# Three gathers of each expert layer cut into 120 and 8 rows, between short copies that turn the ring of DMA engines

## The chip, the cores and the metric

The kernel runs on one core of a Trainium2 chip. The metric is the device time of one execution in microseconds (us); lower is better. The kernel before takes 2239.84 us, the median of three runs (2239.53 to 2241.55). A profile of one execution goes with it: its time was 2241.91 us and the span of its instructions 2240.1 us.

## What is computed

256 tokens of width 1024 pass a first transformer block (three kinds of attention, a gated feed-forward with a short convolution) and then two layers of a second block: attention, and an expert layer ("PEER"). The change touches the expert layer alone. Cut to that:

```python
def peer_ffn(x, w_query, sub_keys, expert_down, expert_up):
    def chunk(xc):                                   # 128 tokens
        q = (xc @ w_query).reshape(PEER_CHUNK, PEER_HEADS, 2, half)
        s = jnp.einsum('thpk,pnk->thpn', q, sub_keys)
        sv, si = lax.top_k(s, PEER_TOPK)             # 16 of 128 keys, twice
        cand = sv[:, :, 0, :, None] + sv[:, :, 1, None, :]
        cidx = si[:, :, 0, :, None] * PEER_N_KEYS + si[:, :, 1, None, :]
        ...
        top_s, sel = lax.top_k(cand, PEER_TOPK)      # 16 of 16 x 16 pairs
        eidx = jnp.take_along_axis(cidx, sel, axis=-1)
        g = jax.nn.softmax(top_s, axis=-1)
        u, vv = expert_down[eidx], expert_up[eidx]
        act = jax.nn.gelu(jnp.einsum('td,thkd->thk', xc, u), approximate=False)
        return jnp.einsum('thk,thkd->td', g * act, vv)
```

Every token takes 8 heads x 16 experts from 16384, and each expert is one row of `experts` with its down and up vectors side by side: 2 x 1024 floats, 8 KB.

## The kernel before

The kernel is written by hand for each engine: a program for SP (weight loads), POOL (gathers and small work), PE (matmuls), ACT and DVE, tied by semaphores. The order within an engine is the order in which its program is written; no planner is involved.

An expert layer works in 16 steps of 16 picks: `STEPS` = 2 tiles of 128 tokens x 8 heads. One step k has two passes c of `RING` = 8 picks each. For one pick of all 128 tokens of a tile, POOL issues one indirect DMA (`gather`, L1098): 128 rows of 8 KB from `experts` into slot r of `ring`, one row to each partition, with the row numbers in a column of `EIDX`. So there are 256 gathers in a layer, 512 in all. What follows for a slot, always in this order:

- DVE waits for `g_landed[r]` and takes the dot of the tokens with the down vectors (L2143 in step 0, L2166 later).
- ACT takes the gelu of it (L1667), times the gate (L1669), and puts it on a diagonal matrix (L1672).
- PE multiplies the diagonal with the up vectors into PSUM (`slot`, L1315) and raises `slot_used[r]`.
- POOL waits for `slot_used[r]` and issues the gather of the same slot for the next pass.

Eight slots thus bound how far POOL runs ahead. Between its dots DVE does the routing of the next step (top-16 of the keys, `paired` and `keyed`), which ends with the row numbers in `EIDX` (L2046) and raises `routed`; `gathers(k, b)` on POOL waits for that once per step. Steps 0 and 1 are written out on POOL, the others are a loop. In the first tile (k under 8) PE also does the rest of the query projections between the slots.

SP loads the weight halves in the order in which they are needed (`reload`, L1039). For the halves of layer 1 it waits, from the second half on, for the last gather of layer 0. After the last gather of a layer, PE closes the sums (L1323, L1327), DVE adds them to x (L484), and the next layer or the store of the result follows. The changed parts are the SP program (L1047 to L1066), `gathers` on POOL (L1102 to L1117), and `step_dve` on DVE (L2154 to L2200).

Of the kernel before, what the change touches and what calls it, by code (L numbers as in the profile page):

```python
# [83 lines left out]
PQ_FIRST = 3  # L84
DOTS_AHEAD = 2
PQ_MIXED = PH - PQ_FIRST
PQ_HELD = range(2 * PQ_FIRST + 1, 2 * PH)
# [66 lines left out]
def build(nc, x_in, wstream, consts, bands, par1, par2, na_bias, experts, out):  # L154
    ctx = ExitStack()
    with ctx:
# [3 lines left out]
        def sem(name):  # L160
            return ctx.enter_context(nc.semaphore(name))
# [12 lines left out]
        ZERO = sb("zero", [P, 512], BF16)  # L174
        EIDX = sb("expert_idx", [P, 2, TOPK], U32)
        GWT = sb("expert_gate", [P, 2, TOPK])
        work = sb("work", [P, 16392])
# [120 lines left out]
        topd_ready, texp_ready, routed, gates_ready = sem("topd_ready"), sem("texp_ready"), sem("routed"), sem("gates_ready")  # L298
        g_landed = [sem(f"g_landed{i}") for i in range(RING)]
        slot_used = [sem(f"slot_used{i}") for i in range(RING)]  # L300
        dots_ready, gelu_ready, w_ready, diag_ready = sem("dots_ready"), sem("gelu_ready"), sem("w_ready"), sem("diag_ready")
# [7 lines left out]

        class Norm:  # L310


            def __init__(self, name):
                self.sq = sem(name + "_squares")
                self.var = sem(name + "_var")
                self.std = sem(name + "_std")
                self.rstd = sem(name + "_rstd")
                self.hn = sem(name + "_normed")
                self.xp = sem(name + "_transposed")
                self.hi = sem(name + "_hi")  # L320
                self.hT = sem(name + "_hT")

        n_attn, n_post, n_ffn = Norm("n_attn"), Norm("n_post"), Norm("n_ffn")
        n_mix, n_peer = Norm("n_mix"), Norm("n_peer")

# [702 lines left out]
        def _(sp):  # L1028
# [13 lines left out]
            with sp.Fori(0, whole) as k:  # L1042
                for s in range(SLOTS):
                    sp.wait_ge(w_lo, k * SLOTS + s + 1)
                    sp.dma_start(W[:, s, :], wstream[k * SLOTS + SLOTS + s]).then_inc(w_landed[s], 16)
            for n in range(SLOTS + whole * SLOTS, HALVES):
                l, local = divmod(n - L_HALF, L_HALVES)  # L1047
                if held(n) is not None:
                    continue
                if n >= L_HALF + L_HALVES and 0 < local < SLOTS:  # L1050
                    sp.wait_ge(g_landed[RING - 1], l * USES * 16)
                reload(n)
                e = local - HELD_BESIDE
                if 0 <= e < len(PQ_HELD):
                    if e == 0:
                        sp.wait_ge(lpT_taken, l * L_FILLS + batches2[-1].values + 1)
                    gains_end = Q_QKN + (e - HELD_ARENA + 1) * HW - Q_GF
                    if gains_end > 0 and e >= HELD_ARENA:
                        sp.wait_ge(n_peer.hn, 4 * l + -(-min(gains_end, D) // GC))
                    sp.dma_start(held_place(e), wstream[L_HALF + l * L_HALVES + 2 * LG_PQ + PQ_HELD[e]]).then_inc(held_landed[e], 16)  # L1060
            sp.wait_ge(x_ready, 3 * LAYERS + 2 * TT - 1)
            sp.wait_ge(g_landed[RING - 1], LAYERS * USES * 16)
# [7 lines left out]
        def _(pool):  # L1070
# [7 lines left out]
            for l in range(LAYERS):  # L1078
# [22 lines left out]

                def gathers(k, b):  # L1102

                    wait_alone(pool, routed, l * ROUTES + k + 1, pool_passed)
                    for c in range(PASSES):
                        for r in range(RING):
                            gather(b, c, r, l * USES + k * PASSES + c)

# [3 lines left out]
                for r in range(RING):  # L1112
                    gather(0, 1, r, l * USES + 1)
                gathers(1, 1)
                with pool.Fori(0, STEPS // 2 - 1) as i:
# [609 lines left out]
        def _(dve):  # L1725
# [146 lines left out]
            for l in range(LAYERS):  # L1872
# [280 lines left out]

                def step_dve(t, k, b, uses, mixed=None, ahead=2):  # L2154

                    rc = Chain(dve, route_step)
                    pairs = paired(rc, k + 1, 1 - b, min((k + 1) // PH, TT - 1) if isinstance(k, int) else t, l * PICKED + k * TOPK + 1) if ahead else None
                    for c in range(PASSES):
# [5 lines left out]
                        for r in range(RING):  # L2164
                            dve.wait_ge(g_landed[r], use * 16 + 16)
                            nc.vector.tensor_tensor_reduce(ring[:, r, 0:D], HN[:, t, :], ring[:, r, 0:D], 1.0, 0.0,  # L2166
                                                           ALU.mult, ALU.add, hd[:, r:r + 1]).then_inc(dots_ready, 1)
                            if c == 0 and ahead:
                                pairs[r]()
                            elif c and r % 2 == 0 and ahead > 1:  # L2170
                                halves[r // 2]()
                            elif mixed:
                                mixed(c, r)
# [22 lines left out]
                for k in range(1, PH):  # L2196
                    def mixed(c, r):
                        if k < PQ_MIXED and r in (1, 3):
                            lo_query(2 * (PQ_FIRST + k) + 1 + r // 2)
                    step_dve(0, k, k % 2, l * USES + k * PASSES, mixed)  # L2200
                with dve.Fori(0, PH // 2 - 1) as i:
# [154 lines left out]
```

## Time and profile before

| what | value |
|---|---|
| median of three runs | 2239.84 us |
| profiled execution: time, span | 2241.91 us, 2240.1 us |
| PE, DVE, ACT, POOL busy | 89%, 72%, 51%, 39% |
| gathers | 512, 536.9 MB, 57.8% of 16 DMA engines' span |
| first expert stage, first to last gather | 734.6 to 1385.6 us |
| second expert stage | from about 1590 to 2232.1 us |

Busy shares are means over very different stages. The slices of the page show two long stretches with the DMA engines full, and these are the expert stages. A DMA share is the mean over 16 engines: 0.06 is one of them at work, 0.12 two.

### The profile page before, as it was taken

How to read it: one execution, taken by the hardware profiler on the slowest of the kernel's cores; microseconds unless marked ns; L12 is line 12 of the kernel's file. 1: busy time of each engine (PE TensorE's matmuls, PEld its weight loads, DVE VectorE, ACT ScalarE, POOL GpSimd, SP SyncE). 2: the span in 40 equal slices, each digit the busy share in tenths (PEclk: the TensorE clock that was granted, in tenths of full speed). 3: DMA queues.
4: the chain of work that ended last, by engine and by line, in shares of the span. 5: the costliest groups of instructions: out<-in, count | busy, mean ns of one | idle time of the engine just before them, and what ended most of it. 6: DMA issues, size and time to landing. Idle time of an engine off the chain costs nothing.

```text
span 2240.1 us, 29611 instructions
## 1 busy us (share of the span) xinstructions
PE 1990.3 (89%) x9760; PEld 1302.1 (58%) x9798; DVE 1609.4 (72%) x3230; ACT 1144.5 (51%) x2534; POOL 874.5 (39%) x557
## 2 busy tenths in 40 slices
PE   9999999999999898977777788999899887778877
PEld 8999899998889644422222223889644432222222
DVE  4566777777787877776777765787887776777774
ACT  4455555545554655454454545565655444444443
POOL 0120000000230355566667663040355566666664
PEclk9999999999999999999999999999999999999999
DMA  7544465665636999999999997736899999999998
GB/s 247 172 132 142 148 184 180 185 189 157 219 119 219 381 421 421 421 421 421 421 418 422 420 421 302 233 116 222 334 421 421 421 421 421 422 422 411 422 421 338
DMA packets 120772, 707.23 MB, mean 316 GB/s; under 512 B 13664, under 2 KB 13920, under 8 KB 55008
## 3 DMA queue, kind: packets, MB, share of 16 engines
q0 software_dynamic: 73728, 536.90, 57.8%
q1 hardware_dynamic: 43488, 157.63, 22.4%
q10 hardware_dynamic: 3456, 11.40, 1.5%
q8 instruction: 57, 0.93, 0.2%
q14 instruction: 43, 0.35, 0.0%
HBM read 704.84 MB, written 1.05 MB: 315 GB/s over the span
## 4 chain that ended last, share of the span: by engine, by line
PE 41%; DMA 25%; POOL 11%; DVE 9%; issue 8%; ACT 6%; POOLq 0%; SPq 0%; DVEq 0%; ACTq 0%
DMA work<-in_experts,expert_idx 24%; PE ps L548 11%; POOL work L1098 10%; PE ps L549 10%; PE ps L550 10%; PE ps L1315 6%; DVE work L2166 2%; DVE weights_lo L533 2%; PE ps L687 1%; ACT L1616 1%; ACT L1667 1%; DMA weights<-in_wstream 1%; ACT arena L1672 1%; DVE work L2143 1%; PE ps L713 1%
## 5 line engine op out<-in xcount | busy, mean ns | idle before, releaser
L1315 PE MATMUL ps<-work,arena 128*128 128x512 f32 x2040 | 989.9, 617 | 216.1 <-ACT arena L1672 212.4
L1098 POOL DMA_INDIRECT work<-in_experts,expert_idx x512 | 790.2, 1543 | 621.2 <-PE ps L1315 291.3
L1315 PEld LDWEIGHTS ps<-work,arena 128*128 128x128 f32 x2040 | 359.0, 191 | 821.0 <-ACT arena L1672 516.2
L2166 DVE CUSTOM_DVE_ANT_0 work<-h_norm,work 128x1024 f32<-128x1024 f32 x480 | 588.1, 1225 | 334.5 <-DMA work<-in_experts,expert_idx 320.2
L1667 ACT ACTIVATE small<-small 128x1 f32<-128x1 f32 x512 | 150.2, 293 | 609.1 <-DVE small L2166 588.0
L533 DVE TENSOR_TENSOR weights_lo<-weights,weights_hi 128x1024 fp32r<-128x1024 f32 x280 | 349.8, 1255 | 152.8 <-ACT weights_hi L528 152.1
L548 PE MATMUL ps<-feat_hi,weights_hi 128*128 128x256 f32 x1528 | 445.3, 291 | 7.6 <-DVE weights_lo L533 5.8
L528 ACT ACTIVATE weights_hi<-weights 128x1024 fp32r<-128x1024 f32 x280 | 295.0, 1056 | 286.0 <-PE ps L550 232.6
L549 PE MATMUL ps<-feat_lo,weights_hi 128*128 128x256 f32 x1528 | 432.8, 283 | 0.0
L550 PE MATMUL ps<-feat_hi,weights_lo 128*128 128x256 f32 x1528 | 432.7, 283 | 0.0
L548 PEld LDWEIGHTS ps<-feat_hi,weights_hi 128*128 128x128 f32 x1528 | 293.3, 192 | 18.1 <-issue 9.3
L549 PEld LDWEIGHTS ps<-feat_lo,weights_hi 128*128 128x128 f32 x1528 | 293.6, 192 | 5.4 <-issue 4.8
L550 PEld LDWEIGHTS ps<-feat_hi,weights_lo 128*128 128x128 f32 x1528 | 293.5, 192 | 0.0
L1087 POOL TENSOR_TENSOR work<-arena,consts 128x640 f32<-128x640 f32 x8 | 13.9, 1769 | 525.3 <-issue 445.8
L1672 ACT ACTIVATE arena<-consts,small 128x128 f32<-128x128 f32 x512 | 205.5, 401 | 16.7
L1669 ACT ACTIVATE small<-small,expert_gate 128x1 f32<-128x1 f32 x512 | 150.7, 294 | 16.7
L754 POOL TENSOR_TENSOR work<-work,small 128x1024 f32<-128x1024 f32 (+2 forms) x26 | 60.0, 2310 | 197.3 <-DVE small L744 197.3
L548 PE MATMUL ps<-weights_hi,feat_hi 128*128 128x256 f32 (+2 forms) x416 | 131.4, 316 | 1.8 <-DVE feat_lo L465 0.9
L549 PE MATMUL ps<-weights_lo,feat_hi 128*128 128x256 f32 (+2 forms) x416 | 128.2, 308 | 0.0
L550 PE MATMUL ps<-weights_hi,feat_lo 128*128 128x256 f32 (+2 forms) x416 | 128.2, 308 | 0.0
L1786 DVE SCALAR_TENSOR_TENSOR work<-ps,params,work 128x254 f32<-128x254 f32 (+1 forms) x128 | 55.8, 477 | 51.8 <-ACT work L1469 47.6
L548 PEld LDWEIGHTS ps<-weights_hi,feat_hi 128*128 128x128 f32 x416 | 79.6, 191 | 7.1 <-DVE weights_lo L533 1.5
(250 smaller groups left out, 1912.1 us busy)
## 6 DMA issues: line engine op xcount, KB each, us to landing
weights<-in_wstream SPq DMA_DIRECT2D x280, 512.0 KB, 4.2
work<-in_experts,expert_idx POOLq DMA_INDIRECT x512
arena<-in_wstream SPq DMA_DIRECT2D x12, 512.0 KB, 6.0
arena<-in_na_bias ACTq DMA_DIRECT2D x6, 512.0 KB, 5.3
params<-in_wstream SPq DMA_DIRECT2D x6, 512.0 KB, 5.9
arena<-in_bias ACTq DMA_DIRECT2D x5, 512.0 KB, 4.6
params<-in_par ACTq DMA_DIRECT2D x2, 576.0 KB, 5.3
params<-in_par ACTq DMA_DIRECT2D x1, 1024.0 KB, 6.7
```

The lines of the kernel that those rows point to most:

```text
L528: nc.scalar.activation(WH[:, n % SLOTS, :], raw(n), ACT.Copy).then_inc(w_hi, 1)
L533: nc.vector.tensor_tensor(WL[:, n % SLOTS, :], raw(n), WH[:, n % SLOTS, :], ALU.subtract).then_inc(w_lo, 1)
L548: nc.tensor.matmul(out, stat[0], mov[0], start=start, stop=False)
L549: nc.tensor.matmul(out, stat[0], mov[1], start=False, stop=False)
L550: return nc.tensor.matmul(out, stat[1], mov[0], start=False, stop=stop)
L754: nc.gpsimd.tensor_tensor(part, part, view(rsum[b.turn][:, r0:r1], [1, r1 - r0], [0, b.width]), ALU.mult).then_inc(A.probs, 1)
L1098: nc.gpsimd.indirect_dma_start(ring[:, r, :], None, experts, bass.IndirectOffsetOnAxis(ap=EIDX[:, b, c * RING + r:c * RING + r + 1], axis= ...
L1315: ins = nc.tensor.matmul(bank(2 * t + h), DIAG[:, r, :], ring[:, r, D + h * 512:D + (h + 1) * 512], start=False, stop=False)
L1667: nc.scalar.activation(ga[:, r:r + 1], hd[:, r:r + 1], ACT.Gelu, scale=rstd[:, t:t + 1]).then_inc(gelu_ready, 1)
L1669: nc.scalar.activation(gw8[:, r:r + 1], ga[:, r:r + 1], ACT.Copy, scale=GWT[:, b, c * RING + r:c * RING + r + 1]).then_inc(w_ready, 1)
L1672: nc.scalar.activation(DIAG[:, r, :], ident, ACT.Copy, scale=gw8[:, r:r + 1]).then_inc(diag_ready, 1)
L2166: nc.vector.tensor_tensor_reduce(ring[:, r, 0:D], HN[:, t, :], ring[:, r, 0:D], 1.0, 0.0, ALU.mult, ALU.add, hd[:, r:r + 1]).then_inc(dots ...
```

## The change

In both layers, three of the 16 gathers of step k=1 are changed: those of the second pass into slots 1, 3 and 5 (`SHARED`). Each is issued as two indirect DMAs, one for 120 rows and one for the other 8 (`SHARED_ROWS`); the 8 have a semaphore of their own per slot, for which DVE waits too. The row numbers of the last 8 partitions are first copied by SP to `REST`, which begins at partition 0. Behind each pair POOL issues a copy of nine short rows (32 bytes each) from `consts` to an unused part of `SMALL`; ahead of the first pair and behind the last it issues a copy of eight such rows. SP waits for all copies at the end. `n_mix` keeps only the three semaphores that it uses.

```diff
+SHARED = (1, 3, 5)
+SHARED_ROWS = 120
+MOVED = 9
+MOVES = 5
...
+        REST = sb("rest_idx", [P - SHARED_ROWS, RING], U32)
...
+            def rest_moved(l):
+
+                sp.wait_ge(routed, l * ROUTES + 2)
+                sp.dma_start(REST[:, :], EIDX[SHARED_ROWS:P, 1, RING:2 * RING]).then_inc(rest_index, 16)
+
             for n in range(SLOTS + whole * SLOTS, HALVES):
                 l, local = divmod(n - L_HALF, L_HALVES)
+                if local == 0 and l:
+                    rest_moved(l - 1)
                 if held(n) is not None:
                     continue
...
+            rest_moved(LAYERS - 1)
+            sp.wait_ge(share_moved, 16 * LAYERS * MOVES)
...
+                def gather_part(rows, index, r, landed):
+
+                    nc.gpsimd.indirect_dma_start(ring[rows, r, :], None, experts,
+                                                 bass.IndirectOffsetOnAxis(ap=index, axis=0)).then_inc(landed, 16)
+
+                def move_share(n, nth):
+
+                    at = 400 + 8 * (l * MOVES + nth)
+                    nc.gpsimd.dma_start(SMALL[0:n, at:at + 8], consts[0:n, 0:8]).then_inc(share_moved, 16)
+
+                def gather_shared(b, c, r, use):
+
+                    wait_alone(pool, slot_used[r], use + 1, pool_passed)
+                    if r == SHARED[0]:
+                        move_share(MOVED - 1, 0)
+                    gather_part(slice(0, SHARED_ROWS), EIDX[0:SHARED_ROWS, b, c * RING + r:c * RING + r + 1], r, g_landed[r])
+                    wait_alone(pool, rest_index, 16 * l + 16, pool_passed)
+                    gather_part(slice(SHARED_ROWS, P), REST[:, r:r + 1], r, rest_landed[SHARED.index(r)])
+                    move_share(MOVED, SHARED.index(r) + 1)
+                    if r == SHARED[-1]:
+                        move_share(MOVED - 1, len(SHARED) + 1)
+
+                def gathers(k, b, shared=()):
...
-                            gather(b, c, r, l * USES + k * PASSES + c)
+                            if c and r in shared:
+                                gather_shared(b, c, r, l * USES + k * PASSES + c)
+                            else:
+                                gather(b, c, r, l * USES + k * PASSES + c)
...
-                gathers(1, 1)
+                gathers(1, 1, SHARED)
...
                         for r in range(RING):
                             dve.wait_ge(g_landed[r], use * 16 + 16)
+                            if shared and c and r in SHARED:
+                                dve.wait_ge(rest_landed[SHARED.index(r)], 16 * l + 16)
```

## Rows read from the trace of the kernel before

**Rows 1.** The page, 40 slices of the span: GB/s that the DMA engines moved.

```profile
GB/s 247 172 132 142 148 184 180 185 189 157 219 119 219 381 421 421 421 421 421 421 418 422 420 421 302 233 116 222 334 421 421 421 421 421 422 422 411 422 421 338
```

**Rows 2.** The page: the chain that ended last, shares of the span by line.

```profile
DMA work<-in_experts,expert_idx 24%; PE ps L548 11%; POOL work L1098 10%; PE ps L549 10%; PE ps L550 10%; PE ps L1315 6%; DVE work L2166 2%; DVE weights_lo L533 2%; PE ps L687 1%; ACT L1616 1%; ACT L1667 1%; DMA weights<-in_wstream 1%; ACT arena L1672 1%; DVE work L2143 1%; PE ps L713 1%
```

**Rows 3.** First stage: window, us, PE, PEld, DVE, ACT, POOL busy, clock, DMA share, GB/s.

```profile
790.00:820.00 30.00, 27.20 (x102) 14.56 (x101) 23.00 (x54) 16.06 (x43) 16.74 (x13) 1.00 1.01 420
1000.00:1370.00 370.00, 293.34 (x611) 106.29 (x611) 259.79 (x642) 179.18 (x493) 240.67 (x148) 0.99 1.01 421
```

**Rows 4.** The same windows at the end of the first expert stage.

```profile
1378.00:1379.00 1.00, 0.89 (x2) 0.49 (x3) 0.79 (x1) 0.06 (x1) 0.00 (x0) 1.00 0.79 328
1379.00:1380.00 1.00, 1.00 (x3) 0.19 (x1) 0.44 (x2) 0.49 (x2) 0.00 (x0) 1.00 0.22 90
1380.00:1381.00 1.00, 0.51 (x2) 0.30 (x2) 0.32 (x1) 0.50 (x2) 0.00 (x0) 1.00 0.12 49
1381.00:1385.00 4.00, 3.51 (x8) 1.06 (x6) 2.15 (x4) 1.51 (x5) 0.00 (x0) 1.00 0.07 29
```

**Rows 5.** The same windows at the end of the second expert stage.

```profile
2227.00:2228.00 1.00, 0.94 (x2) 0.49 (x3) 0.84 (x1) 0.01 (x1) 0.00 (x0) 1.00 0.12 49
2228.00:2232.00 4.00, 3.02 (x7) 0.87 (x5) 1.62 (x4) 1.98 (x6) 0.00 (x0) 1.00 0.05 23
```

**Rows 6.** Layer 0's last dot and its sum: start us, us, instruction, idle before.

```profile
1385.65 1.22 DVE L2166 CUSTOM_DVE_ANT_0 work<-h_norm,work 128x1024 f32<-128x1024 f32 x1 [1.24 <-DMA work<-in_experts,expert_idx]
...
1389.40 0.69 DVE L484 TENSOR_TENSOR x<-x,ps 128x512 f32<-128x512 f32 x1 [2.52 <-remote]
```

**Rows 7.** All issues of gathers: duration in ns, least, median, most.

```profile
L1098 POOL DMA_INDIRECT work<-in_experts,expert_idx x512: 932/1730/1980, 734.6 to 2217.4; - x171
```

**Rows 8.** Instructions of DVE and POOL around step 1, second pass, layer 0.

```profile
787.35 1.23 DVE L2166 CUSTOM_DVE_ANT_0 work<-h_norm,work 128x1024 f32<-128x1024 f32 x1 [0.39 <-DMA work<-in_experts,expert_idx]
787.56 1.83 POOL L1098 DMA_INDIRECT work<-in_experts,expert_idx  x1 [0.69 <-issue]
...
789.69 0.94 POOL L1098 DMA_INDIRECT work<-in_experts,expert_idx  x1 [0.30 <-issue]
...
792.71 1.54 POOL L1098 DMA_INDIRECT work<-in_experts,expert_idx  x1 [0.78 <-PE ps L1315]
...
805.87 0.94 POOL L1098 DMA_INDIRECT work<-in_experts,expert_idx  x1 [0.78 <-PE ps L1315]
```

**Rows 9.** Layer 1's issues into slots 1 and 6.

```profile
1639.92 1.80 POOL L1098 DMA_INDIRECT work<-in_experts,expert_idx  x1 [0.79 <-PE ps L1315]
...
1653.35 0.94 POOL L1098 DMA_INDIRECT work<-in_experts,expert_idx  x1 [0.78 <-PE ps L1315]
```

**Rows 10.** Windows, gathers' issues alone: window, us, POOL busy, clock, DMA share, GB/s.

```profile
792.70:805.80 13.10, 6.78 (x5) 1.00 1.01 420
1639.90:1653.30 13.40, 7.30 (x5) 1.00 1.01 422
```

**Rows 11.** DVE: the row numbers of step 1, and slot 6's dots in both layers.

```profile
773.73 0.23 DVE L2046 TENSOR_SCALAR expert_idx<-arena,small 128x16 uint32<-128x16 f32 x1
...
820.31 1.23 DVE L2166 CUSTOM_DVE_ANT_0 work<-h_norm,work 128x1024 f32<-128x1024 f32 x1 [1.15 <-DMA work<-in_experts,expert_idx]
...
1667.06 1.23 DVE L2166 CUSTOM_DVE_ANT_0 work<-h_norm,work 128x1024 f32<-128x1024 f32 x1 [1.18 <-DMA work<-in_experts,expert_idx]
```

**Rows 12.** Issues of DMAs: KB each, us to landing; the last within 1060 to 1180.

```profile
result<-x ACTq DMA_DIRECT2D x1, 256.0 KB, 2.0
params<-in_par ACTq DMA_DIRECT2D x2, 12.0 KB, 4.9
params<-in_par ACTq DMA_DIRECT2D x1, 12.0 KB, 6.7
```

**Rows 13.** SP's loads at the start of the first expert stage, and ACT's first use.

```profile
726.67 15.89 SPq L1039 DMA_DIRECT2D weights<-in_wstream  x5
...
1368.01 1.04 ACT L528 ACTIVATE weights_hi<-weights 128x1024 fp32r<-128x1024 f32 x1
```

More of the change, by code:

```diff
@@ L299, in build @@
         g_landed = [sem(f"g_landed{i}") for i in range(RING)]
+        rest_landed = [sem(f"rest_landed{r}") for r in SHARED]
+        rest_index, share_moved = sem("rest_index"), sem("share_moved")
         slot_used = [sem(f"slot_used{i}") for i in range(RING)]
@@ L308, in build, with __init__ @@
         pool_passed, dve_passed = sem("pool_waits_passed"), sem("dve_waits_passed")
-        class Norm:
+        class Turns:
             def __init__(self, name):
+                self.xp = sem(name + "_transposed")
+                self.hi = sem(name + "_hi")
+                self.hT = sem(name + "_hT")
+        class Norm(Turns):
+            def __init__(self, name):
+                super().__init__(name)
                 self.sq = sem(name + "_squares")
@@ L318, in __init__ @@
                 self.hn = sem(name + "_normed")
-                self.xp = sem(name + "_transposed")
-                self.hi = sem(name + "_hi")
-                self.hT = sem(name + "_hT")
         n_attn, n_post, n_ffn = Norm("n_attn"), Norm("n_post"), Norm("n_ffn")
-        n_mix, n_peer = Norm("n_mix"), Norm("n_peer")
+        n_mix, n_peer = Turns("n_mix"), Norm("n_peer")
         def root_table(col):
@@ L1100, in gather @@
                         bass.IndirectOffsetOnAxis(ap=EIDX[:, b, c * RING + r:c * RING + r + 1], axis=0)).then_inc(g_landed[r], 16)
-                def gathers(k, b):
+                def gather_part(rows, index, r, landed):
[15 more added lines that the diff above has]
+                def gathers(k, b, shared=()):
                     wait_alone(pool, routed, l * ROUTES + k + 1, pool_passed)
@@ L2152, in _, with step_dve @@
                 rc.restart()
-                def step_dve(t, k, b, uses, mixed=None, ahead=2):
+                def step_dve(t, k, b, uses, mixed=None, ahead=2, shared=False):
                     rc = Chain(dve, route_step)
@@ L2199, in mixed @@
                             lo_query(2 * (PQ_FIRST + k) + 1 + r // 2)
-                    step_dve(0, k, k % 2, l * USES + k * PASSES, mixed)
+                    step_dve(0, k, k % 2, l * USES + k * PASSES, mixed, shared=k == 1)
                 with dve.Fori(0, PH // 2 - 1) as i:
```

## Prediction

> **What bounds the kernel now.** I read the page first, then windows, then single instructions. The slices show two long stretches in which the 16 DMA engines move a steady 421 GB/s [rows 1]. They are the two expert stages. On the chain, transfers of the gathers (24%) and POOL's issues of them (10%) are the largest parts that belong to these stages [rows 2]; there are 512 gathers, 256 in each. The slices don't show the share of the engines, so I asked for windows: from 790 to 1370 us it is 1.01 at 420 to 421 GB/s whatever the other engines do, with DVE, ACT and POOL well short of full [rows 3]. A gather is 128 rows of 8 KB, 1.05 MB, so 2.49 us at 421 GB/s. One of 16 engines moves 26.3 GB/s, so a row costs its engine 8192 B / 26.3 GB/s = 0.31 us.
>
> The reader should look hardest at how a stage ends. The engines don't stop together: the share is full until 1378 us, then 0.79, 0.22, 0.12, and then 0.07 at 29 GB/s for four whole microseconds [rows 4]. 0.06 is one engine of 16, and 25 GB/s is one engine's rate. One engine is thus some 4.3 us (1381.3 to 1385.6) behind the second-latest, and 6.6 us behind the rest. The second stage ends alike: 0.12 in 2227 to 2228, then 0.05 at 23 GB/s to 2232 [rows 5], a lead of some 3.5 us. Each gather's semaphore needs all its engines, so the last dot (1385.65) starts when that one engine is done, and PE's last slots, the closing matmuls and the residual sum follow without a gap [rows 6]. Both tails are on the path with their full length.
>
> Taking rows away from that one engine shortens the stage until the next engine is last; taking them from any other engine shortens nothing.
>
> **What the change does, part by part.** In each layer three of 256 gathers (step k=1, second pass, slots 1, 3, 5) are cut into 120 rows and 8 rows. The reading under which the numbers 120, 8, 9 make sense: 120 rows go eight each to 15 engines, 8 rows one each to 8 engines, and the next transfer starts at the next engine in a ring of 16. Then 15+8+9 = 32 brings the ring back to its place after each cut gather, and the copies of eight ahead and behind (8+8 = 16) turn it half round and back. All three gathers then leave out the same engine, which carries 1 row of the 128 each time, and seven of its neighbours carry 9. Relief: 3 x 7 = 21 rows, 21 x 0.31 = 6.5 us per layer. Price: seven engines get 3 rows, 0.9 us, more per layer. No row of this trace shows a transfer on fewer than 16 engines, so this is a reading and not a measurement.
>
> The Trainium skill (DMA: Bandwidth & Descriptors, "Why a DMA increments its semaphore by 16 and not by 1") states this rule: k, the largest divisor up to 16 of the outer dimension, and k consecutive engines from a round-robin cursor. It adds that some direct copies issued by GpSimd go out on 16 engines anyway; if the short copies did, they wouldn't turn the ring, the three gathers would relieve three different engines by 7 rows each, and the sum would be that of the second rival. No run shows either yet.
>
> *The gain if the relieved engine is the late one.* It is bounded by the second-latest: 4.3 us in the first stage, 3.5 us in the second, each less 0.9 if that engine is among the seven: 5.9 to 7.8 us in both layers [rows 4, 5]. A second bound comes from POOL. An engine can only run ahead into gathers that are already issued.
>
> *POOL.* Eight transfers are added per layer between the issue of slot 1 and that of slot 6: three gathers of 8 rows and five copies. A gather's issue takes 0.93 us at least, 1.73 in the median, 1.98 at most [rows 7]; the long ones are those that meet a dot on DVE (787.56 for 1.83 beside the dot at 787.35 to 788.58) [rows 8], and 0.30 us lies between two when nothing is waited for [rows 8]. The trace has no copy issued by POOL and no 8-row gather; from above I bound them by 1.98, from below by the 0.30 alone. From 792.71 to 805.87 POOL now spends 6.8 us in five issues and 5 x 0.30 between them, so 13.2 - 6.8 - 1.5 = 4.9 us are free (waits for PE, the most of them); in the second layer, 1639.92 to 1653.35, 13.4 - 7.3 - 1.5 = 4.6 [rows 8 to 10]. Slot 6 is then issued late by 8 x (0.93 + 0.30) - 4.9 = 5.0 us (5.3), by 8 x (1.73 + 0.30) - 4.9 = 11.3 us (11.6) at the median, and not at all if a short transfer costs POOL under 0.3. I take the 0.93: it is nearest for lists a sixteenth as long, though those that meet a dot will stretch.
>
> *The cushion.* Slot 6, issued at 805.87, has its dot at 820.31: 14.4 us later; in the second layer 1653.35 to 1667.06, 13.7 us [rows 8, 9, 11]. With nothing queued a gather would need 2.49 us of data and a fixed part. From the 256 KB result that part is 1.4 us (2.0 less 0.6 of data) and POOL's 0.94 comes on top; from the 12 KB load it is 4.9, which counts from the issue [rows 12]. So 4.8 to 7.4 us, and I take the middle, 6.1. The cushion is 8.3 us (7.6). Subtracting the lateness gives what the late engine can gain: 8.3 - 5.0 = 3.3 us and 7.6 - 5.3 = 2.3 us. Both lie under the bounds above. Sum: -5.6 us. If the late engine isn't relieved the same cushion says what POOL costs: nothing until it is late by more than 8.3 us.
>
> *Parts at nothing.* The index copy REST waits on SP for the second routing. EIDX is written at 773.73 [rows 11], a 12 KB load in the same kind of stretch landed after 6.7 us [rows 12], and POOL asks for it after 793: over 12 us of cover; without it POOL would wait that long. Behind SP's wait in layer 0 stands the first weight half of layer 1, now issued within the five issues from 726.67 to 742.56, then after 774; it is first read at 1368.01 [rows 13], so some 590 us remain, and its 0.5 MB costs the engines 1.2 us in either place. Behind the wait at the end of the program stands only the result. DVE asks three times more per layer whether a cut gather has landed, ahead of dots that stand behind 0.39 to 1.18 us of idle time [rows 8, 11]; ACT and PE queue behind the dot as before. The five copies of 32 bytes a row move 2.7 KB together in two layers. The shorter class for one norm removes names of semaphores and no instruction.
>
> **Sum.** The profiled execution has a span of 2240.1 us and a time of 2241.9; the median of the runs is 2239.84. -5.6 against the first is -5.6 against the median: 2234.2 us. Its own range is 2232.0 (both bounds full, -7.8) to 2236.5 (one more stretched issue or two in each layer).
>
> **Rivals.** (1) POOL becomes the bound. At the median issue it is late by 11.3 and 11.6 us, the cushion is 8.3 and 7.6, and all engines run dry for 3.0 and 4.0 us: +7.0 us, 2246.8. The mechanism is the dot that holds up POOL in half of each 2.49 us; it decides from 1.35 us a short transfer on ((8.3 + 4.9)/8 = 1.65 with its gap). For it: the five issues of the window take 1.36 us on average in layer 0 and 1.46 in layer 1 [rows 10]. Against it: when POOL has a backlog it also falls into free stretches, and lists are short. Chance 0.18.
> (2) The relieved engine isn't the late one, or three different ones are relieved. The trace doesn't number engines, so nothing in it says which is late. Then 0, or +0.9 per layer when the late one is among the seven: 2239.8 to 2241.7. Chance 0.22. The Trainium skill (same page, "Latency and other measured facts") says that engines 7 and 15 are usually the slow ones under transfers of this queue; with a ring that starts at 0 and is turned by eight, the engine left out is 7. The trace agrees that one engine is late, not with which. Without the turn it would be 15.
> (3) A cut gather is slower than a whole one. In a whole gather the 16 engines keep a steady 421 GB/s even when one is microseconds behind; a list dealt out otherwise may have two engines writing where one did. From zero up to twice the time of three gathers, 3 x 2.49 = 7.5 us a layer: 2240 to 2255; I take half of it with 1 us of gain left, 2246. The Trainium skill (SBUF — State Buffer, "Door 1: The DMA port swizzle") ties the rate to how many of 16 ports the partitions reach at a time; eight neighbouring partitions of each engine reach fewer at a time than the present deal. By it the sum would be up to +15 us; no row shows it. Chance 0.12.
> (4) Between forecast and rival 1: POOL stretches partly (1.2 us each) and the gain is used up: 2237 to 2241. Chance 0.12.
> The forecast keeps 0.36.
>
> **Range and chances.** From full bounds at 2232 to the first rival at 2247, 2231.0 to 2247.0; outside are the worse half of rival 3 and the upper end of issues at 1.98 us. About 0.2% (4.5 us) can be told from no change. Faster by more: the forecast and a little of rival 4, 0.37. Within: rivals 2 and 4 and the weak end of 3, 0.37. Slower: rivals 1 and 3, 0.26.
>
> **What the profile after would show.** Right: the windows at the ends of both stages have a shorter stretch at 0.06, with two engines (0.12) close together; POOL's eight added issues near 0.9 us; share 1.0 throughout 790 to 830 us. Rival 1: windows under 0.9 between 810 and 830, POOL's issues at 1.7 with no wait for PE. Rival 2: tails of 4.3 and 3.5 us or more as before, with the share full throughout. Rival 3: share full, GB/s under 400 near 810. Wrong altogether: a stage that ends earlier with an unchanged tail, or one whose length changes far from the cut gathers.

## The result and the profile after

The changed kernel takes 2267.78 us (median of 4 runs, 2267.32 to 2270.56) beside 2239.78 us of the kernel before on the same chip: +28.0 us, a ratio of 1.0126 with an interval of 1.0108 to 1.0143. That is slower, 33.6 us from the forecast of 2234.2 and 21 us past the upper end of the range. The profiled execution has 2267.7 us and a span of 2265.9. The medians below are of runs in the usual state; one run of the kernel with two halves of 64 rows, 2319.48 us at a mean granted clock of 0.843, is left out for that.

| | before | after |
|---|---|---|
| median of the runs, us | 2239.78 | 2267.78 |
| profiled span, us | 2240.1 | 2265.9 |
| last dot of the first expert stage starts, us | 1385.65 | 1398.78 |
| layer 1's first gather of step k=1 starts, us | 1622.10 | 1633.78 |
| last dot of the second expert stage starts, us | 2232.11 | 2257.87 |

The first stage gives away 13.1 us. Between the stages 1.4 us come back, so that layer 1's step k=1 begins 11.7 us late. The second stage ends 25.8 us late and so gives away 14.1 us.

The page of the changed kernel, 40 slices of the span, GB/s that the DMA engines moved:

```profile
GB/s 246 170 136 146 137 186 185 189 181 170 210 112 233 408 321 421 421 421 421 420 418 421 422 422 292 224 121 223 372 309 421 421 421 421 421 422 419 422 422 337
```

Against [rows 1] two slices stand out, 321 and 309 where 421 and 421 stood. They are those in which the cut gathers lie, the 15th (793 to 850 us) and the 30th. Everything else in the two stages moves at the old rate. Windows say where in the slice. Columns as in [rows 3]: window, us, PE, PEld, DVE, ACT, POOL busy, granted clock, share of the DMA engines, GB/s.

```profile
790.00:802.00 12.00, 11.53 (x49) 6.86 (x50) 9.67 (x25) 8.02 (x20) 8.61 (x9) 1.00 1.02 421
802.00:831.00 29.00, 21.36 (x56) 9.30 (x54) 12.26 (x28) 7.32 (x21) 12.34 (x11) 0.82 1.02 227
831.00:1000.00 169.00, 148.92 (x443) 69.90 (x442) 124.57 (x305) 86.06 (x233) 94.48 (x67) 0.97 1.01 421
...
1661.00:1691.00 30.00, 19.89 (x56) 8.70 (x54) 12.07 (x27) 7.09 (x20) 12.48 (x12) 0.89 1.03 213
```

The kernel before in the same two windows:

```profile
802.00:831.00 29.00, 25.38 (x74) 11.49 (x73) 21.55 (x51) 13.52 (x37) 15.81 (x13) 1.00 1.01 421
1661.00:1691.00 30.00, 27.90 (x104) 15.01 (x103) 23.01 (x57) 17.86 (x47) 17.58 (x12) 1.00 1.01 421
```

These rows are the whole result. The share of the DMA engines is full in both kernels, so nobody fails to give them work. They move half of it: 227 and 213 GB/s. The bytes that are missing from 29 us at 227 in place of 421 are worth 29 x (1 - 227/421) = 13.4 us, where the stage's end shows 13.1; for the second, 30 x (1 - 213/421) = 14.8, where it shows 14.1. A row of 8 KB keeps its engine busy for 8192 B x 16 x 1.02 / 227 GB/s = 0.59 us instead of 0.31. Everything behind DMA has less to do in the window: DVE 12.3 us instead of 21.6. TensorE's granted clock averages 0.82 in the window (before: 1.00, its level of 2.4 GHz), where PE has 56 matmul records instead of 74; PE isn't what the stage waits for.

POOL's issues from the cut gathers on (start us, us, instruction, idle before; L1120 is a whole gather, L1126 a part of a cut one, L1132 a short copy):

```profile
792.56 0.55 POOL L1132 DMA_DIRECT2D small<-in_consts  x1 [0.47 <-issue]
793.41 1.13 POOL L1126 DMA_INDIRECT work<-in_experts,expert_idx  x1 [0.30 <-issue]
794.84 0.90 POOL L1126 DMA_INDIRECT work<-in_experts,rest_idx  x1 [0.30 <-PE ps L1362]
795.74 0.57 POOL L1132 DMA_DIRECT2D small<-in_consts  x1
...
808.02 1.48 POOL L1120 DMA_INDIRECT work<-in_experts,expert_idx  x1 [0.30 <-issue]
809.80 0.96 POOL L1120 DMA_INDIRECT work<-in_experts,expert_idx  x1 [0.30 <-issue]
814.19 1.85 POOL L1120 DMA_INDIRECT work<-in_experts,expert_idx  x1 [3.43 <-PE ps L1362]
818.63 0.93 POOL L1120 DMA_INDIRECT work<-in_experts,expert_idx  x1 [2.59 <-PE ps L1362]
823.97 1.38 POOL L1120 DMA_INDIRECT work<-in_experts,expert_idx  x1 [4.41 <-PE ps L1362]
```

Slot 6 is issued at 808.02, 2.15 us after its time in the kernel before [rows 8]. After slot 7 POOL waits 2.6 to 4.4 us at a time in these rows for a slot to come free. POOL has time to spare, and it is the slots, and behind them the transfers, that are late.

The ends of the stages after, the same columns:

```profile
1393.00:1394.00 1.00, 0.51 (x2) 0.27 (x2) 0.17 (x1) 0.65 (x2) 0.00 (x0) 1.00 0.20 82
1394.00:1395.00 1.00, 1.00 (x3) 0.41 (x3) 1.00 (x2) 0.00 (x0) 0.00 (x0) 1.00 0.12 49
1395.00:1398.00 3.00, 2.52 (x6) 0.68 (x4) 1.29 (x4) 1.38 (x5) 0.00 (x0) 1.00 0.07 27
...
2253.00:2254.00 1.00, 1.00 (x3) 0.52 (x4) 1.00 (x1) 0.00 (x0) 0.00 (x0) 1.00 0.08 33
2254.00:2258.00 4.00, 3.03 (x7) 0.90 (x6) 1.52 (x5) 1.98 (x6) 0.00 (x0) 1.00 0.05 20
```

One engine alone at 27 and 20 GB/s for three to four us, as in [rows 4, 5]. The change was to take rows from an engine, and the tail that one engine makes has kept its length.

### The profile page after: what moved, and what is told of

Its sections match the earlier page's. It is cut to its first block, busy times and chain, and to the rows that moved or that the text cites. A ratio compares the mean times of both kernels' runs of the same rounds, so it can differ in the third digit from the quotient of the medians.

```text
span 2265.9 us, 29675 instructions
## 1 busy us (share of the span) xinstructions
PE 2009.5 (89%) x9798; PEld 1309.1 (58%) x9798; DVE 1610.2 (71%) x3230; ACT 1144.7 (51%) x2534; POOL 875.8 (39%) x573
## 3 DMA queue, kind: packets, MB, share of 16 engines
HBM read 704.84 MB, written 1.05 MB: 312 GB/s over the span
## 4 chain that ended last, share of the span: by engine, by line
PE 39%; DMA 26%; POOL 11%; DVE 10%; issue 8%; ACT 6%; POOLq 0%; SPq 0%; DVEq 0%; ACTq 0%
DMA work<-in_experts,expert_idx 24%; POOL work L1120 10%; PE ps L561 10%; PE ps L563 10%; PE ps L562 10%; PE ps L1362 6%; DVE weights_lo L546 2%; DVE work L2215 2%; DMA weights<-in_wstream 1%; PE ps L700 1%; ACT L1714 1%; DVE work L2190 1%; ACT L1663 1%; ACT arena L1719 1%; ACT weights_hi L541 1%
## 5 line engine op out<-in xcount | busy, mean ns | idle before, releaser
L1362 PE MATMUL ps<-work,arena 128*128 128x512 f32 x2040 | 1008.0, 628 | 225.4 <-ACT arena L1719 224.1
L1120 POOL DMA_INDIRECT work<-in_experts,expert_idx x506 | 773.0, 1528 | 641.2 <-PE ps L1362 332.3
L1362 PEld LDWEIGHTS ps<-work,arena 128*128 128x128 f32 x2040 | 366.8, 195 | 840.8 <-ACT arena L1719 530.7
```

The costliest lines, as they stand in the source:

```text
L1120: nc.gpsimd.indirect_dma_start(ring[:, r, :], None, experts, bass.IndirectOffsetOnAxis(ap=EIDX[:, b, c * RING + r:c * RING + r + 1], axis= ...
L1362: ins = nc.tensor.matmul(bank(2 * t + h), DIAG[:, r, :], ring[:, r, D + h * 512:D + (h + 1) * 512], start=False, stop=False)
```

## The experiments

The theory after the result: a list of 120 or 8 rows is dealt to the engines so that they hinder each other, and the cut alone costs the time (the third rival's mechanism, at more than its bound). The rivals: the short copies or the waits do it; POOL does it; the number 120 (15 engines in place of 16) does it.

### The cut and the copies apart

The first kernel keeps the three cut gathers and drops all copies:

```diff
-MOVES = 5
+MOVES = 0
-            sp.wait_ge(share_moved, 16 * LAYERS * MOVES)
-                    if r == SHARED[0]:
-                        move_share(MOVED - 1, 0)
-                    move_share(MOVED, SHARED.index(r) + 1)
-                    if r == SHARED[-1]:
-                        move_share(MOVED - 1, len(SHARED) + 1)
```

> The changed kernel without its five short copies per layer: three gathers cut into 120 and 8 rows, nothing else. The changed kernel is 28 us slower than the one before, and its DMA engines are full (1.0) at 197 to 280 GB/s from 802 to 831 us. Theory D (the deal: a cut list gives each engine other partitions, so that engines get in each other's way in writing, and rows take 0.6 us in place of 0.31): all or most of the loss stays, 2260 to 2268 us, rows at 0.6 us for 20 to 30 us in both layers. Theory C (the copies, whose packets of 32 bytes get between the rows): within 3 us of 2240. Theory P (POOL's added issues): half the loss, 2250 to 2256.

The second keeps copies, the index copy REST and POOL's waits, and gathers whole:

```diff
+                def gather_shared(b, c, r, use):
+                    if r == SHARED[0]:
+                        move_share(8, 0)
+                    gather(b, c, r, use)
+                    wait_alone(pool, rest_index, 16 * l + 16, pool_passed)
+                    move_share(9, SHARED.index(r) + 1)
+                    if r == SHARED[-1]:
+                        move_share(8, 4)
```

> The three gathers whole, with the five short copies per layer, the index copy and POOL's wait for it kept. Theory D: no loss beyond what POOL's five issues take from the cushion, 2239 to 2242 us, GB/s stays at 421 around 800 to 830. Theory C: 2260 us or more. Theory P: 5 x 0.9 us a layer less the 4.9 us that POOL has free, so also within 3 us of 2240; this run cannot tell D from P, the first one does.

Without copies: 2270.82 us beside 2240.65, ratio 1.0136 (1.0119 to 1.0153). With copies and no cut: 2241.28, ratio 1.0002 (0.9992 to 1.0012). The window of the kernel without copies:

```profile
802.00:831.00 29.00, 15.33 (x25) 5.28 (x24) 11.05 (x26) 6.66 (x19) 7.28 (x8) 0.82 1.02 210
```

The windows of the kernel with copies alone:

```profile
802.00:831.00 29.00, 25.34 (x74) 11.42 (x73) 21.74 (x50) 13.23 (x36) 16.84 (x15) 1.00 1.01 421
1661.00:1691.00 30.00, 28.41 (x105) 15.34 (x104) 22.25 (x57) 17.70 (x45) 17.87 (x12) 1.00 1.01 421
```

The whole loss is in the cut, and the copies, REST and the added wait of POOL cost nothing that can be told. (DVE's added waits are not in the second kernel.) The kernel without copies lies 2.8 us above theory D's range.

The packets of the trace carry no engine number, but on full engines their times tell them apart. In the first layer of the kernel with copies alone, the first copy's eight short packets start at eight moments between 802.31 and 803.67 us. The second's come at the same spacing 2.48 to 2.50 us later, which is one gather, and have a ninth among them. So the 43 packets of a layer's five copies (8 x 5 + 3) lie on the same eight engines and a ninth. A direct copy from POOL therefore begins at the same engine each time. That it leaves alone the place in the ring where the next gather begins is concluded from this; no packet shows it.

### Other sizes of the parts

```diff
-SHARED_ROWS = 120
+SHARED_ROWS = 64
```

> The same three gathers cut into 64 and 64 rows, no copies. Both parts divide by 16, so all 16 engines can carry 4 rows each and no engine is left out. Theory D: engines still get other partitions than in a whole gather, so rows take about 0.6 us and the loss stays within a factor of two of 28 us: 2254 to 2285. Rival U (uneven loads: fewer than 16 engines at work, some with 9 rows and one with 1, break the even flow): no loss, 2238 to 2243, rows stay at 0.31 us.

and, the same edit with 112:

> The same three gathers cut into 112 and 16 rows, no copies: 7 rows and 1 row for each of 16 engines. Theory D: 16 partitions dealt one to each engine put four engines on each place, so packets of up to 1.2 us appear, and the loss is near that of 120 and 8: 2250 to 2275. Rival U: no loss, 2238 to 2243.

Both without copies. 64 + 64 rows: 2271.11 us, ratio 1.0138 (1.0117 to 1.0158). 112 + 16: 2262.94, ratio 1.0095 (1.0078 to 1.0112). The window of 64 + 64 rows:

```profile
802.00:831.00 29.00, 19.90 (x48) 8.89 (x47) 12.13 (x28) 6.98 (x20) 8.74 (x9) 0.76 1.02 220
```

The same window with 112 + 16 rows:

```profile
802.00:831.00 29.00, 18.54 (x53) 8.30 (x52) 13.97 (x33) 8.49 (x25) 10.58 (x10) 0.94 1.02 243
```

So it isn't the 15 engines: two halves of 64 rows, which by the same reading put four rows on each of 16 engines, run as slowly. Every cut tried costs much: 30.5 us for 64 + 64, 28.0 and 30.2 for 120 + 8 with and without copies, 22.3 for 112 + 16. Why 112 + 16 costs less wasn't tried.

### How many cuts, and how far apart

One cut gather in each layer, without copies:

```diff
-SHARED = (1, 3, 5)
+SHARED = (1,)
```

> One gather per layer (slot 1) cut into 120 and 8 rows in place of three, no copies. With three the stretch at half rate lasted some 29 us, which is the work of the cut gathers and of the two whole ones between them (5 gathers and the 8 rows, at 2 x 2.49 us each). Theory D1 (whole gathers are slowed too while engines work at a cut one beside them): one cut gather halves the rate for some 5 to 6 us and costs 2.5 to 3.5 us per layer, 2246 to 2248 us. Theory D2 (each cut gather costs a third of the loss, 4.4 to 5 us per layer): 2249 to 2251 us. Theory D3 (one is enough to bring the engines out of step for a long time): over 2255 us.

Three that follow one another:

```diff
-SHARED = (1, 3, 5)
+SHARED = (1, 2, 3)
```

> Three gathers per layer cut into 120 and 8 rows, but those of slots 1, 2 and 3, with no whole one between them, and no copies. Theory D1: the slow stretch holds the three cut gathers and no whole one: 15 to 19 us at half rate, a loss of 8 to 9.5 us per layer: 2256 to 2260 us. Theory D2: as with slots 1, 3 and 5: 2266 to 2271 us.

One cut: 2249.74 us beside 2240.5, ratio 1.0039 (1.0025 to 1.0053). Three neighbours: 2260.84, ratio 1.0085 (1.0068 to 1.0102), 0.8 us above D1's range. The one cut costs 4.6 us a layer, more than D1 expected; its time alone lies in D2's range. But by D2 the three neighbours would cost three times as much, 27.7 us, and they cost 20.3. So D1's mechanism holds, at a higher price. The slow stretch of layer 0 with one cut:

```profile
802.00:811.00 9.00, 5.97 (x14) 2.19 (x12) 2.74 (x9) 2.42 (x7) 3.91 (x4) 1.00 1.00 218
```

The same with three neighbours, and what follows it:

```profile
803.00:822.00 19.00, 11.19 (x22) 3.84 (x20) 7.47 (x19) 4.47 (x13) 7.18 (x6) 0.91 1.02 220
822.00:850.00 28.00, 25.13 (x96) 14.85 (x96) 21.06 (x50) 14.87 (x38) 12.68 (x10) 0.94 1.01 421
```

In the slow stretches 9 us x 218 = 2.0 MB move with one cut, 19 x 220 = 4.2 MB with three neighbours, 29 x 227 = 6.6 MB with three spaced ones. In gathers of 1.05 MB that is 1.9, 4.0 and 6.3. A run of cut gathers thus slows itself and about one whole gather more: 1 + 1, 3 + 1, and three times 1 + 1. This is the part that the prediction lacked. While a whole gather shares the engines with a cut one, the bytes of both come at half rate, and in the change each of the three cut gathers has such a neighbour.

### The rate of each list by itself

The kernel before, with nine bursts of eight gathers once its result is stored, when DVE, ACT and PE are at rest. Each burst is three whole gathers and five of one kind. In front of them it has short direct copies of growing length behind the last gathers of each stage, to find which engine is late.

```diff
+BURSTS = ((WHOLE,), (slice(0, 120),), (slice(0, 64),), (slice(0, 32),), (slice(0, 16),), (slice(0, 64, 4),), (slice(0, 8),), (slice(0, 112),), (slice(0, 120), WHOLE))
...
+            for i, kinds in enumerate(BURSTS):
+                for r in range(RING):
+                    picked(WHOLE if r < 3 else kinds[r % len(kinds)], r)
+                pool.wait_ge(burst, 16 * RING * (i + 1))
```

> The kernel before, with 15 short copies behind its last gathers (seven in layer 0, eight in layer 1, of 2, 4 to 14 and 1, 3 to 15 rows), and, once the result is stored, nine bursts of eight gathers each: three whole ones to fill the queue and five of 128, 120, 64, 32, 16, 16 with every fourth partition, 8 and 112 rows, and of 120 and whole in turn. It measures the cost of a deal by itself, with DVE, ACT and PE at rest; only the times of rows in the bursts count. Theory D, in the form that neighbouring four partitions share one place to write and each engine takes a contiguous share: rows at 0.31 us whole, at 0.6 us for 120, 112, 64 and 32 rows (two engines on a place), at 1.2 us for 16 and 8 neighbouring rows (four on a place), at 0.6 us for 16 rows on every fourth partition. Rival U (uneven load): 0.31 us everywhere, or slow for 120 and 8 alone. A further rival H (the reads of rows from memory get slow in another order): 16 rows take the same on neighbouring partitions as on every fourth. The short copies tell by their number behind the last row which engine of 16 is the late one, if copy of n rows goes to the first n engines.

It takes 2464.97 us in its one run, bursts and all. The windows inside each burst, in the order 128, 120, 64, 32, 16 neighbouring rows, 16 rows on every fourth partition (two windows), 8 rows, 112, and 120 and 128 in turn:

```profile
2248.00:2258.00 10.00, 0.00 (x0) 0.00 (x0) 0.00 (x0) 0.00 (x0) 0.00 (x0) 0.50 1.01 427
2272.00:2290.00 18.00, 0.00 (x0) 0.00 (x0) 0.00 (x0) 0.00 (x0) 0.00 (x0) 0.50 1.02 232
2307.00:2316.00 9.00, 0.00 (x0) 0.00 (x0) 0.00 (x0) 0.00 (x0) 0.00 (x0) 0.50 1.01 206
2331.00:2335.00 4.00, 0.00 (x0) 0.00 (x0) 0.00 (x0) 0.00 (x0) 0.00 (x0) 0.50 1.03 207
2349.00:2355.00 6.00, 0.00 (x0) 0.00 (x0) 0.00 (x0) 0.00 (x0) 0.00 (x0) 0.50 0.89 104
2367.00:2368.00 1.00, 0.00 (x0) 0.00 (x0) 0.00 (x0) 0.00 (x0) 0.00 (x0) 0.50 1.24 418
2368.00:2369.00 1.00, 0.00 (x0) 0.00 (x0) 0.00 (x0) 0.00 (x0) 0.00 (x0) 0.50 0.97 197
2384.00:2385.00 1.00, 0.00 (x0) 0.00 (x0) 0.00 (x0) 0.00 (x0) 0.00 (x0) 0.50 0.80 41
2402.00:2418.00 16.00, 0.00 (x0) 0.00 (x0) 0.00 (x0) 0.00 (x0) 0.00 (x0) 0.50 1.01 228
2433.00:2449.00 16.00, 0.00 (x0) 0.00 (x0) 0.00 (x0) 0.00 (x0) 0.00 (x0) 0.50 1.02 263
```

The last two columns are the reading. A full share with 427 GB/s for whole lists, and a full share with 206 to 232 for 120, 112, 64 and 32 rows. Sixteen neighbouring rows fall to a quarter, 104 at a share of 0.89. The same number of rows on every fourth partition goes back to half: the window from 2367 us still holds the whole gathers (418), and the next one has 197 at 0.97, so a row takes 8192 B x 16 x 0.97 / 197 GB/s = 0.65 us. These two bursts take the same rows of the table (`EIDX[0:n]`) and differ only in the partitions that they write, so rival H (the reads) is refuted. It isn't the number of rows, nor the number of engines that have some: it is which partitions are written at the same time. Burst 9 has 2 cut and 3 whole gathers in turn. One after the other at 232 and 427 GB/s they would take 8.5 + 7.4 us for 5.11 MB, 322 GB/s, and the window has 263: the whole ones suffer too, as in the kernel. PE, DVE, ACT and POOL are at 0.00 in all these windows, so none of them is the cause. The eight rows of the seventh burst are over soon. At a share of 0.80 they come at 41 GB/s, so a row takes 8192 B x 16 x 0.80 / 41 GB/s = 2.6 us, twice the 1.2 that theory D gave. If lists of eight rows in turn fall on the other eight engines, all 16 write the same eight partitions, which would double it; that is argued.

The Trainium skill (SBUF — State Buffer, "Door 1: The DMA port swizzle") states that the rate goes by how many of 16 ports the written partitions reach, four neighbours and the four that lie 32 higher sharing one, at about 27.2 GB/s a port. Its estimates for the first 64 and the first 32 partitions are about 218 GB/s each and for the first 16 about 109; the bursts have 206, 207 and 104, so the trace agrees. By it every fourth partition of the first 64 reaches 8 ports (estimate 218; the burst has 197). The Trainium skill (DMA: Bandwidth & Descriptors, "The descriptor swizzle") adds that in a list of 128 each engine has a port for itself. If 120 rows go eight neighbours to an engine instead, engines 0 and 4 begin on the same port, as do 1 and 5, and only half of the ports work at a time: again an estimate of 218, where the burst has 232. Which partitions an engine writes isn't in the record, so of this last step the rate is shown and the layout is argued.

Behind the late stretch of the stages, the short copies show the late engine's number. Taken that a copy of n rows touches engines 0 to n - 1, counted from the one where all copies begin, the number of copies on the late engine gives its place. In layer 0 (n = 2, 4 ... 14) six of the seven copies have a packet of 16 bytes behind its last row (1384.57 to 1384.63 us), so it has number 2 or 3; in layer 1 (n = 1, 3 ... 15) six of eight (2229.44 to 2229.51), so 3 or 4. Together: number 3.

### Is the relief real?

If the direct copies don't turn the ring, the change never did what it says. Here the copies become gathers of short rows, which should take their place in the ring as the long ones do. With the change's lengths, 8 ahead and 9 behind, the engine left out is number 7:

```diff
-                    nc.gpsimd.dma_start(SMALL[0:n, at:at + 8], consts[0:n, 0:8]).then_inc(share_moved, 16)
+                    nc.gpsimd.indirect_dma_start(SMALL[0:n, at:at + 8], None, experts.rearrange("e (a b) -> (e a) b", b=8),
+                                                 bass.IndirectOffsetOnAxis(ap=EIDX[0:n, 1, RING:RING + 1], axis=0)).then_inc(share_moved, 16)
```

> The changed kernel, with indirect copies of short rows (32 bytes a row out of the expert table) in place of its direct ones. In the run with copies alone the direct ones always used the same engines, one row each from the first on, so they cannot have turned the ring for the gathers; indirect ones of 8 and 9 rows should, as the 120 and 8 rows do. By the number of short packets behind the last row the late engine is the fourth (number 3). Turned by 8 the cut gathers leave out number 7 three times. Both theories: the slow stretches stay (28 us at half rate in each layer), no relief for the late engine, its tail of about 4 us stays: 2264 to 2272 us.

With 4 ahead, 9 behind each and 12 at the end it is number 3, the late one:

```diff
-                        move_share(MOVED - 1, 0)
+                        move_share(4, 0)
...
-                        move_share(MOVED - 1, len(SHARED) + 1)
+                        move_share(12, 4)
```

> The same with indirect copies of 4 ahead of the three cut gathers, 9 behind each, 12 behind the last, so that the three leave out number 3, the late one. Theory R (relief is real, 21 rows or 6.5 us, and the loss by the deal comes on top): the tail of a lone engine is gone or under 1.5 us at the end of both stages, and the time is 3 to 8 us under that of the run turned by 8. Theory N (the bound is the place that is written, not the engine, so others that write the late engine's partitions only share its delay): tails and time as in the run turned by 8, within 3 us.

Number 7 left out: 2266.03 us beside 2240.74, ratio 1.012 (1.0103 to 1.0137). Number 3 left out: 2257.56, ratio 1.0081 (1.0064 to 1.0098), 8.5 us less; the two intervals don't meet. The end of the first stage with number 7 left out:

```profile
1392.00:1393.00 1.00, 0.49 (x2) 0.30 (x2) 0.23 (x1) 0.60 (x2) 0.00 (x0) 1.00 0.14 57
1393.00:1394.00 1.00, 1.00 (x3) 0.38 (x2) 1.00 (x2) 0.00 (x0) 0.00 (x0) 1.00 0.06 25
1394.00:1397.00 3.00, 2.53 (x6) 0.68 (x4) 1.24 (x3) 1.46 (x5) 0.00 (x0) 1.00 0.07 27
```

The same with number 3 left out:

```profile
1392.00:1393.00 1.00, 0.50 (x2) 0.30 (x2) 0.28 (x1) 0.55 (x2) 0.00 (x0) 1.00 0.33 139
1393.00:1394.00 1.00, 1.00 (x3) 0.38 (x2) 0.95 (x2) 0.02 (x1) 0.00 (x0) 1.00 0.27 115
1394.00:1395.00 1.00, 0.62 (x2) 0.00 (x0) 0.00 (x0) 0.94 (x3) 0.00 (x0) 1.00 0.08 33
```

In the first the lone engine at 25 and 27 GB/s stays for four us. In the second it is gone, and the stage ends within two us of several engines (115 GB/s is some four of them). In the second stage of that kernel the last three us have 164, 49 and 8 GB/s, where the kernel with number 7 left out has 25 GB/s for four us (2252 to 2256). So taking rows from the late engine does shorten the stage. It also shows that the short gathers turn the ring, for only their lengths differ between the two kernels. But the slow stretch stays. Here it is for number 3 left out:

```profile
802.00:832.00 30.00, 18.85 (x49) 8.79 (x48) 11.37 (x27) 6.33 (x19) 10.60 (x12) 0.77 1.02 220
```

Layer by layer the two profiles can be compared less well: the second saves 2.5 us up to the last dot of layer 0 and 8.0 in what follows, while the two lose some 2 us more and 1 us less in their slow stretches. I take 4 us a layer from the medians, and leave the split open.

Last, one cut gather a layer with number 3 left out (4 ahead, 9 behind, 12 at the end):

```diff
-SHARED = (1, 3, 5)
+SHARED = (1,)
```

> One gather per layer (slot 1) cut into 120 and 8 rows, with the indirect short copies that make it leave out number 3, the late engine: 4 rows ahead, 9 and 12 behind. One cut gather without copies cost 9 us in both layers (2249.7 us) and left the tails of 4 us; three that relieve the late engine by 21 rows cost 17 us, 8.5 less than three that relieve another. If relief goes by rows, 7 rows are 2.2 us a layer: 2244 to 2247 us, and a lone tail of about 2 us. If the relief only works when the late engine gets wholly clear of the others: 2248 to 2251 us. Either way over the 2240 of the kernel before; under 2240 would make this the better kernel.

2246.38 us beside 2240.35, ratio 1.0024 (1.0014 to 1.0033); without the turn the one cut took 2249.74. By the medians, each against its own runs of the kernel before, relief of 7 rows a layer gave 9.2 - 6.0 = 3.2 us of 2 x 7 x 0.31 = 4.3. The two intervals overlap, so this number isn't clear of the noise. The end of the first stage:

```profile
1384.00:1385.00 1.00, 0.49 (x3) 0.05 (x1) 0.00 (x0) 0.84 (x3) 0.00 (x0) 1.00 0.12 49
1385.00:1386.00 1.00, 1.00 (x3) 0.52 (x4) 0.97 (x1) 0.00 (x0) 0.00 (x0) 1.00 0.12 49
1386.00:1387.00 1.00, 0.94 (x3) 0.11 (x1) 0.26 (x2) 0.64 (x3) 0.00 (x0) 1.00 0.10 41
```

Two engines (49 GB/s) now end together, where one stood alone. In the second stage one engine still ends alone, from 2233 us on:

```profile
2233.00:2234.00 1.00, 0.84 (x2) 0.49 (x3) 0.74 (x1) 0.11 (x1) 0.00 (x0) 1.00 0.06 25
2234.00:2235.00 1.00, 1.00 (x3) 0.19 (x1) 0.49 (x2) 0.44 (x2) 0.00 (x0) 1.00 0.08 33
```

That is the tail of about 2 us that was expected. Even with the smallest number of cuts, aimed at the right engine, the cut costs (9.2 us) more than its relief brings. No version tried is faster than the kernel before.

| kernel | cuts a layer | engine left out, by the ring | time, us | against before |
|---|---|---|---|---|
| as changed | 3 spaced | three different | 2267.78 | +28.0 |
| no copies | 3 spaced | three different | 2270.82 | +30.2 |
| copies alone | 0 | none | 2241.28 | +0.6 |
| 64 + 64 rows, no copies | 3 spaced | none | 2271.11 | +30.5 |
| 112 + 16 rows, no copies | 3 spaced | none | 2262.94 | +22.3 |
| three neighbours | 3 | three different | 2260.84 | +20.3 |
| one cut | 1 | another in each layer, not 3 | 2249.74 | +9.2 |
| ring turned by 8 | 3 spaced | 7 | 2266.03 | +25.3 |
| ring turned by 4 | 3 spaced | 3 | 2257.56 | +16.8 |
| ring turned by 4 | 1 | 3 | 2246.38 | +6.0 |

## Why the prediction was wrong

**What bounds the kernel.** Right. The transfers are the bound, one engine makes the tail, and what slows the transfers shows at the end almost one to one (13.4 us by the windows, 13.1 by the last dot). The leads were read too long, for the prediction took the start of the last dot for the end of the last row. In the packets the late engine's last row ends at 1385.18 and the second-latest engine's at 1381.54: 3.6 us, not 4.3. In the second stage it is 3.1, not 3.5.

**The reading of 120, 8 and 9.** Half right. Twenty-one rows off the late engine bring about 4 us a layer, close to the four us for which the lone engine stays when number 7 is left out. Number 3, left out, takes the tail away. But the change didn't relieve it: after the change the tail stands as before [rows 4, 5], and the direct copies always begin at the same engine. If they leave the ring unturned, three different engines were relieved by 7 rows each. That is the second rival, with a chance of 0.22; as no packet shows which engines were left out, it is argued. The Trainium skill's exception for direct copies (DMA: Bandwidth & Descriptors, "Why a DMA increments its semaphore by 16 and not by 1") stood in the prediction and I gave it no more weight than that. The packets, always on the same engines, agree with it. And had the copies turned the ring, the engine left out would have been number 7, which isn't the late one: 2266.03 us. Either way the relief was missed. The Trainium skill's remark that engines 7 and 15 are usually the slow ones (DMA: Bandwidth & Descriptors, "Latency and other measured facts") doesn't hold here, where number 3 is late.

**The step that failed: the rate of a cut gather.** The forecast took a row at 0.31 us whatever list it came from. The only rows were those of whole gathers [rows 3], and from them "the 16 engines keep a steady 421 GB/s" was carried to lists of which no row existed. The third rival had the mechanism and its sign (share full, GB/s under 400 near 810), but a chance of 0.12 and too small a size. "Up to twice the time of three gathers", 7.5 us a layer, counts the cut gathers alone. Measured were 13.1 and 14.1, since three spaced cuts slow six gathers. With that number, 6 x 2.49 = 14.9 us, the term would have been right to within 2 us. The range ended at 2247, which left out even the worse half of the rival as it stood. An unknown price on the one resource that bounds the stage should have set the range's upper end, at 2255 by my own numbers and at 2270 with the neighbours counted.

**POOL.** Too dear. Eight added issues at 0.93 + 0.30 made slot 6 late by 5.0 us; it was 2.15 in the first layer. A short direct copy takes POOL 0.55 to 0.58 us and often follows without a gap, and the part of 8 rows takes 0.90 in the median of six (once 1.94), nearly what a whole gather takes in free time. The nearest row (0.93) fitted the gathers and not the copies. The first rival (0.18) needed 1.35 us on average and is refuted by POOL's waits for PE behind slot 6. The cushion of 8.3 us was never used up.

**Parts at nothing.** Right. With copies, REST and POOL's waits but no cut, the time is the old one to about 0.1% (ratio 0.9992 to 1.0012). DVE's added waits weren't tried by themselves.

## What to carry to other kernels

A full share of the DMA engines doesn't mean full speed: read GB/s beside it, and work out what one row costs its engine. Where a stage is bound by transfers, as here, keep each one across all 128 partitions. A cut that leaves the bytes the same can double the time of a row, and it drags the whole transfer beside it along. A trick that balances engines must be paid for in rows that are worth it, and first one has to know which engine is late: short transfers of growing length behind the last long one tell it.

## What was not expected of the hardware

- 120, 112, 64 and 32 rows of 8 KB are gathered at 206 to 232 GB/s, 128 rows at 427. Sixteen neighbouring rows: 104; sixteen on every fourth partition: 197.
- Two halves of 64 rows, issued one behind the other, don't make a whole: the kernel with them has 220 GB/s in the stretch and is 30.5 us slower.
- A cut gather slows about one whole gather more: slow stretches of 1.9, 4.0 and 6.3 gathers for one cut, three neighbours and three spaced.
- POOL's direct copies begin at the same engine each time, while its gathers of short rows turn the ring: with them, 4 ahead and 12 at the end in place of 8 and 8 are worth 8.5 us.
- One engine, number 3, is the late one in both stages. Why it is late wasn't tried and stays open.
